# Query weights of a two-layer model kernel: ten units loaded into four raw buffers and six borrowed ones, or all through the four raw buffers

## The reference

```python
def peer_ffn(h, wq, keys, u, v):
    def block(xt):                      # 128 tokens at a time
        q = (xt @ wq).reshape(-1, PEER_HEADS, 2, PEER_HALF)
        s = jnp.einsum('thpc,hpnc->thpn', q, keys)
        sv, si = lax.top_k(s, PEER_TOPK)
        ...                             # top 16 of the 16 x 16 pairs: expert ids and gates
        ue = jnp.take(u, eid, axis=0)
        act = jax.nn.gelu(jnp.einsum('thkd,td->thk', ue, xt), approximate=False)
        ve = jnp.take(v, eid, axis=0)
        return jnp.einsum('thk,thkd->td', gate * act, ve)
```

## Time and profile before

| what | value |
|---|---|
| median of 3 runs | 3023.57 us (3021.9 to 3032.02) |
| the profiled execution: its own time, its span | 3024.71 us, 3022.7 us |
| granted TensorE clock, mean of the span | 0.993 |
| busy: PE, DVE, ACT, POOL | 89%, 57%, 29%, 18% |
| HBM read | 856.56 MB |
| chain that ended last | PE 58%, DMA 31%, DVE 5% |

### The profile page before, as it was taken

How to read it: one execution, slowest core, us unless ns; L and a number is a source line. 1 busy time by engine, 2 the same in 40 slices (tenths; PEclk the granted TensorE clock), 3 DMA queues, 4 the chain that set the end, 5 groups by cost and what they waited for, 6 DMA issues and landing times.

```text
span 3022.7 us, 32757 instructions
## 1 busy us (share of the span) xinstructions
PE 2677.6 (89%) x12366; PEld 1919.2 (63%) x12366; DVE 1725.7 (57%) x2229; ACT 883.1 (29%) x979; POOL 546.7 (18%) x532
## 2 busy tenths in 40 slices
PE   8999999987777777777777779999999999999998
PEld 8999888732222222222222338998788888888887
DVE  5556557645555555555565464545656655655445
ACT  5433441211111011111111014533434444444444
POOL 0000003544333333343344430000000000000000
PEclk9999999999999999999999999999999999999999
DMA  7554578999999999999999994544464555555554
GB/s 254 175 168 154 181 237 337 391 421 421 422 421 422 422 422 422 422 422 422 422 422 422 409 359 161 172 142 156 143 215 149 187 193 184 192 190 185 194 194 153
DMA packets 222587, 859.97 MB, mean 285 GB/s; under 512 B 17696, under 2 KB 24224, under 8 KB 149792
## 3 DMA queue, kind: packets, MB, share of 16 engines
q0 software_dynamic: 73728, 536.90, 43.0%
q1 hardware_dynamic: 148768, 321.80, 31.9%
HBM read 856.56 MB, written 2.10 MB: 284 GB/s over the span
## 4 chain that ended last, share of the span: by engine, by line
PE 58%; DMA 31%; DVE 5%; issue 3%; ACT 2%; POOL 1%; POOLq 0%; DVEq 0%; ACTq 0%
DMA vb<-in_peer_v,vidx 28%; PE PS L549 11%; PE PS L2270 7%; PE PS L2489 7%; PE PS L551 5%; PE PS L578 4%; PE PS L582 4%; PE PS L580 4%; PE PS L596 4%; PE PS L600 4%; PE PS L598 4%; DMA ub<-in_peer_u,uidx 2%; DVE wl L462 1%; DVE ub L1633 1%; DMA raw<-in_peer_v,vidx 1%
## 5 line engine op out<-in xcount | busy, mean ns | idle before, releaser
L2270 PE MATMUL PS<-vb,diag 128*128 128x512 f32 x1920 | 886.8, 606 | 285.7 <-DMA vb<-in_peer_v,vidx 285.7
L462 DVE TENSOR_TENSOR wl<-raw,wh 128x2048 fp32r<-128x2048 f32 x266 | 609.7, 2292 | 651.9 <-ACT wh L457 651.5
L1633 DVE CUSTOM_DVE_ANT_0 ub<-ub,RES 128x2048 f32<-128x2048 f32 x256 | 586.4, 2292 | 498.3 <-DMA ub<-in_peer_u,uidx 497.8
L2270 PEld LDWEIGHTS PS<-vb,diag 128*128 128x128 f32 x1920 | 347.3, 190 | 824.5 <-issue 532.0
L457 ACT CAST wh<-raw 128x2048 fp32r<-128x2048 f32 x266 | 507.0, 1906 | 766.3 <-PE PS L551 254.2
L549 PE MATMUL PS<-XHL,wh 128*128 128x512 f32 x1376 | 477.2, 394 | 0.7 <-DVE wl L462 0.7
L813 POOL DMA_INDIRECT ub<-in_peer_u,uidx x256 | 278.2, 1087 | 591.1 <-DVE uidx L1617 476.9
L551 PE MATMUL PS<-XHL,wl 128*128 128x256 f32 x1376 | 381.2, 277 | 0.0
L813 POOL DMA_INDIRECT vb<-in_peer_v,vidx x240 | 244.5, 1019 | 628.5 <-PE PS L2270 599.3
L578 PE MATMUL PS<-XHL,wh 128*128 128x256 f32 x1152 | 329.1, 286 | 4.4 <-DVE XHL L1333 2.6
L582 PE MATMUL PS<-XHL,wl 128*128 128x256 f32 x1152 | 326.6, 284 | 0.0
(11 more groups left out here) (384 smaller groups left out, 2436.7 us busy)
## 6 DMA issues: line engine op xcount, KB each, us to landing
raw<-in_w_in SPq DMA_DIRECT2D x112, 1024.0 KB, 5.1
raw<-in_w_ffn_gate SPq DMA_DIRECT2D x44, 1024.0 KB, 5.2
raw<-in_w_ffn_up SPq DMA_DIRECT2D x44, 1024.0 KB, 5.2
raw<-in_w_ffn_down SPq DMA_DIRECT2D x44, 1024.0 KB, 4.8
raw<-in_w_out SPq DMA_DIRECT2D x32, 1024.0 KB, 5.1
raw<-in_peer_wq SPq DMA_DIRECT2D x10, 1024.0 KB, 6.9
wq_early<-in_peer_wq SPq DMA_DIRECT2D x6, 1024.0 KB, 8.1
ub<-in_peer_u,uidx POOLq DMA_INDIRECT x256, 16.4
```

The source lines that it names most:

```text
L462: dve.tensor_tensor(wl[u % 2][:], raw[u][:], wh[u % 2][:].bitcast(F32), ALU.subtract).then_inc(lo_full[u % 2], 1)
L1633: dve.tensor_tensor_reduce(ub[k % RING][:], ub[k % RING][:], RES[:, tb, :], 1.0, 0.0, ALU.mult, ALU.add, dots[:, tb, k:k + 1]).then_inc(S. ...
L2270: m = pe.matmul(PS[:, 4 * tb + b, :], diag[:, k, :], vb[k % RING][:, b * W:(b + 1) * W], start=False, stop=False, skip_group_check=True)
```

## The change

The helper `wq_buf` and the six borrowed buffers are gone. All of slabs 1, 2 and 3 go to `raw[u]`, and unit u of slab j waits for the use of unit u of slab j - 1 (`q_used` at least 4 (j - 1) + u + 1). The two loads of the second layer behind them wait for `q_used` 13 and 14, where they waited for 15 and 16. What is computed, and its order on TensorE, DVE, ACT and POOL, is the same.

```diff
-    wq_early = [at(f"wq_early{k}", kb, [UC, W]) for k, kb in enumerate((32, 48, 40, 56, 80, 88))]
...
-    def wq_buf(j, u):
-
-        if j == 1:
-            return wq_early[u]
-        if j == 2 and u < 2:
-            return wq_early[UNITS + u]
-        return raw[(u + 2) % UNITS]
...
-        for u in range(UNITS):
-            c = (u % 2) * 2 * UC
-            sp.wait_ge(lo_full[u % 2], (S_IN2 - 1) * 2 + u // 2 + 1)
-            sp.dma_start(narrow(raw[u]), wq[:, c:c + 2 * UC, (u // 2) * 2 * P:(u // 2 + 1) * 2 * P]).then_inc(raw_whole[u], 16)
-        for j in range(1, 4):
+        for j in range(4):
             for u in range(UNITS):
-                if j == 1:
-                    sp.wait_ge(w_free[u // 2], S_IN2 * 2)
-                elif j == 2 and u < 2:
-                    sp.wait_ge(S.out_half, 2)
+                if j == 0:
+                    c = (u % 2) * 2 * UC
+                    sp.wait_ge(lo_full[u % 2], (S_IN2 - 1) * 2 + u // 2 + 1)
+                    sp.dma_start(narrow(raw[u]), wq[:, c:c + 2 * UC, (u // 2) * 2 * P:(u // 2 + 1) * 2 * P]).then_inc(raw_whole[u], 16)
                 else:
-                    sp.wait_ge(q_used, UNITS * (j - 2) + u - 1 if j == 2 else (3, 4, 11, 12)[u])
-                sp.wait_ge(raw_whole[u], 16 * j)
-                sp.dma_start(wq_buf(j, u)[:], wq[:, u * UC:(u + 1) * UC, j * W:(j + 1) * W]).then_inc(raw_whole[u], 16)
+                    sp.wait_ge(q_used, UNITS * (j - 1) + u + 1)
+                    sp.dma_start(raw[u][:], wq[:, u * UC:(u + 1) * UC, j * W:(j + 1) * W]).then_inc(raw_whole[u], 16)
         w_in2 = w_view(inp["w_in_2"])
         for u in range(2):
-            sp.wait_ge(q_used, UNITS * 4 - 1 + u)
+            sp.wait_ge(q_used, UNITS * 3 + u + 1)
             load_unit(sp, S_IN2, u, w_in2[:, u * UC:(u + 1) * UC, 4 * W:5 * W])
...
-                        m = pe.matmul(cm_out(j % 2)[:, t, :], wq_buf(j, u)[:, c, t * P:t * P + P], XF[:, d, :],
+                        m = pe.matmul(cm_out(j % 2)[:, t, :], raw[u][:, c, t * P:t * P + P], XF[:, d, :],
```

## The result

The changed kernel is slower. Beside each other on one chip the medians are 3038.04 us (3034.64 to 3048.48, 7 runs) against 3022.64 us (3019.7 to 3032.02, 7 runs), +15.4 us; the ratio is 1.0054, with a 95% interval of 1.0040 to 1.0068. The forecast was 3040 us, range 3030 to 3049. The profiled execution took 3038.04 us with a span of 3036.3 us, 13.6 us longer than before.

A forecast was written before the change was run, and what follows sets the result against it. The prediction took DMA bandwidth (420 to 422 GB/s) as the bound from 586 us, its start set by TensorE's query product; +24.4 us lateness less 7.0 us given back, about +17 on 3023.6, gave 3040 us, range 3030 to 3049.

The forecast's parts named there:

- The binding view: TensorE's query product and POOL's u gathers end within 2.5 us at the first v gather; then DMA bandwidth binds.
- part 1: Query load issues: those at 487.23 and 494.58 us keep their times, and slab 1 runs as before, ending at 523.
- part 2: Load queue beside the gathers: turns by packet, one load landing every 11.7 us, bounds 3.3 and 12.3 us.
- rival A: Gather stretch, bytes only: loads use gaps and catch up, 2.4 MB too many cost +6 us, 3030 us; chance 0.17.
- part 3: TensorE's query product starves on slabs 2 and 3 and ends at 606.3 instead of 581.9 us, 24.4 us later.
- The clock: TensorE after waits of 3 to 5 us: slower clock worth 1.7 us, nothing charged on the path, kept for the range.
- part 4: The u gathers paced by DVE: last dot ends 3 us later, last u issue at 581, hidden behind TensorE.
- part 5: Start of the v gathers: idle DMA engines after the late start give back 7 us.
- The sum: Whole kernel: +24.4 us of TensorE lateness less 7.0 us given back, +17.4 us, called +17.
- Rival B: Query loads keep up with TensorE, which still ends at 581.9 us: -3 us as a middle, 3020 us; chance 0.06.
- rival C: Last two query loads also land 11.7 us apart, with lower clock: TensorE 33 us later, +26 us, 3050 us; chance 0.15.

The follow-up runs named there:

- e7: Kernel before, loads unchanged, with TensorE doing unit 0 of slab 3 four times instead of once; 3049.9 us, ratio 1.0053.
- e1: Changed kernel with the loads of slabs 1 to 3 in 8 KB packets instead of 2 KB, same bytes; 3040.6 us, ratio 1.0054.
- e9: Changed kernel with units 1 and 3 of slabs 2 and 3 loaded by ACT in a third DMA queue; 3041.8 us, ratio 1.0037.
- e4: Kernel before, slab 3's last two units loaded into freed split buffers, second-layer loads issued some 30 us earlier; 3026.0 us, ratio 0.9994.
- e3: Kernel before, slab 1 still early, slabs 2 and 3 through raw buffers only, second-layer loads at q_used 13 and 14; 3032.2 us, ratio 1.0015.
- e2: Changed kernel with the loads of slabs 1 to 3 in 1 KB packets instead of 2 KB, same bytes; 3050.0 us, ratio 1.0079.
- e5: Changed kernel with the two second-layer loads waiting for q_used 15 and 16 again; 3047.3 us, ratio 1.0051.
- e10: Changed kernel with two u gathers in flight instead of four in steps 0 and 1; 3083.4 us, ratio 1.0170.

## Why the prediction was right, step by step

- **The binding view** was right: two paths meet at the first v gather, and behind it everything is set by 422 GB/s. e7 shows it alone.
- **Issue times of the loads (part 1)** held to within a microsecond, and slab 1 was not late. The landings from the earlier trace rows repeated themselves: 500.0 and 511.7 us. (The two issues that the prediction read there were units 0 and 1 of slab 3, and not of slabs 2 and 3, which changes nothing.)
- **Service (part 2)** had the right law and one wrong premise. I took 11.7 us a load, as if the gather queue always held a packet. Measured from 500.0 us to 592.6 us it was 10.3 us over nine intervals, in an uneven mix (11.7, 11.7, 8.3, 12.0, 11.7, 6.1, 11.8, 8.6, 10.8 us): with both queues full it is 11.7 to 12.0 us, and where the gathers run short, the loads catch up (the packet counts above), which was rival A's argument.
- **The end of the queue (part 3)** went by another path than the forecast's. I had the ninth load at 592.5 us, the tenth nearly alone 3.3 us behind it, and two units back to back, to 606.3 us. The ninth landed at 581.8 us, the tenth 10.8 us behind it at 592.6 us, since u gathers were still in flight, and TensorE waited for it and did one slow unit, to 601.4 us. So the ninth load was 10.7 us early and the tenth only 3.4 us, and an error of 4.9 us at the end hides a larger one before it.
- **The clock (part 3)** I priced rightly and placed wrongly. I charged nothing since the waits before the last two units would be under 1 us (the forecast's own landings make it 1.1 us before the ninth, with 1.7 us of clock in the unit ahead, and 2.8 us without); the last was 3.64 us, and the last unit took 8.78 instead of 7.07 us. The Trainium skill, TensorE: Matmul & The Clock Gate, section Part 1, says that an idle TensorE is throttled to half its clock; the granted clock of 0.81 over that unit agrees. TensorE's lateness came to 19.5 us, not 24.4 us (20.2 us in D, since the first gather started 0.65 us earlier).
- **The other path (part 4)** slipped more than the 3 us that I gave it. The last dot product started at 593.11 us, 5.7 us later counted from the first u gather. It stayed hidden in the changed kernel. In e1 and e9, with TensorE on time or nearly so, the same bytes cost 9.1 and 9.2 us by way of the gathers. Those runs give the loads larger packets or a second queue, and so more of the engines, so they suggest, and don't show, that rival A's price is a floor of this change and not an alternative to it. A's +6 us was low in any case: it took 420 GB/s as the ceiling of 482 to 582 us, and the stretch carried 411, 413 and 408 GB/s (changed, e1, e9), which leaves room for 3 MB and not 3.9.
- **What comes back (part 5)** was 5.6 and 5.3 us, not 7.
- **The sum** was +24.4 - 7.0 = +17.4 us, measured +20.2 - 5.6 = +14.6 us at the end of the stretch, +13.6 us in the span and +15.4 us in the medians. The part on the loads' service and the part on what comes back erred in opposite directions, and the medians move by several us for another reason (last section), so that 3038.0 us came within 2 us of the 3040 forecast is partly luck.
- **Rival B** had the loads keep up. In e1 they did, and it was not faster even then, since the gathers pay. Of **rival C**, the wait before the last unit and its lower clock did come, but not the size: the loads landed 10 us apart and not 11.7, and N grew by 14.6 us and not 26. Its condition came half true: the last two loads landed 8.6 and 10.8 us behind the ones before them, where C had 11.7 us twice.

## What to carry to other kernels

A load that is moved into a stretch where the DMA engines are busy has two prices: its own bytes, paid by whoever shares the engines (9 us here for six loads of 1.05 MB, in e1 and e9), and its lateness, paid by the engine that waits for it. The two overlap: the changed kernel, where the loads were late, lost 10 and 15 us in all. Queues that all hold work shared the engines packet for packet here, so a queue with 2 KB packets beside one with 8 KB packets got a fifth of the bytes, and the law of the queues gives the slowest service, not the mean: look also at how often the other queue is empty. Look for the room in the stretch, not only for the distance between issue and use: a queue of three loads turned 13 us into 33 us. Buffers that are idle a little before such a stretch are worth filling then, even if they are another stage's, and in e4 such buffers also let loads of the next stage leave the saturated stretch.

## What was not expected of the hardware

One stage has two speeds, which no change here touches. In the second layer's gated MLP TensorE is busy for 100 of 100 us in every profile, but does 578 or 579 matmuls in 100 us in some executions and 567 to 569 in others. The kernel before, and e3 (columns as in the earlier trace rows; the DMA rate goes with it):

```profile
2400.00:2500.00 100.00, 100.00 (x579) 87.47 (x578) 61.56 (x58) 46.56 (x29) 0.00 (x0) 1.00 0.58 189
```

```profile
2401.00:2501.00 100.00, 100.00 (x568) 86.77 (x567) 60.12 (x57) 44.85 (x28) 0.00 (x0) 1.00 0.57 182
```

The granted clock is 1.00 in both. The mean 128x512 matmul there takes 394 ns in the one and 399 ns in the other, and from the end of N to the end of the span e2, e3 and e5 to e10 need 1220.3 to 1221.7 us, and before, changed, e1 and e4 1211.6 to 1212.6 us. These 9 us explain a good part of why one kernel's runs lie up to 15 us apart (3019.5 to 3034.5 us for the kernel before, 24 runs), and why a change of 5 us is visible in a profile's stretch and not in the medians. Their cause is open.
